# A hybrid block with a product-key expert layer on one core: the chosen experts' weights added into their table by GpSimd's indirect transfers

## The reference

```python
PEER_HEADS, PEER_N_KEYS, PEER_TOPK = 8, 128, 16      # 128 * 128 = 16384 experts

def peer_ffn(h, w_q, sub_keys, u_tab, v_tab):         # for 128 tokens hb at a time
    q = (hb @ w_q).reshape(128, 8, 2, 128)
    sc = jnp.einsum('thcd,hcnd->thcn', q, sub_keys)
    s1, i1 = lax.top_k(sc[:, :, 0], 16)
    s2, i2 = lax.top_k(sc[:, :, 1], 16)
    cand_s = s1[..., :, None] + s2[..., None, :]      # 256 candidates
    cand_i = i1[..., :, None] * 128 + i2[..., None, :]
    top_s, pos = lax.top_k(cand_s, 16)
    idx = jnp.take_along_axis(cand_i, pos, axis=-1)
    g = jax.nn.softmax(top_s, axis=-1)
    act = jax.nn.gelu(jnp.einsum('thkd,td->thk', u_tab[idx], hb))
    return jnp.einsum('thk,thkd->td', g * act, v_tab[idx])
```

## Time and profile before

| | us |
|---|---|
| median of 3 runs | 3407.14 |
| lowest, highest | 3405.34, 3407.44 |
| the profiled execution, its own time | 3407.45 |
| span of its trace | 3405.7 |
| PE busy | 3253.8 |
| DVE busy | 1926.9 |
| ACT busy | 1232.9 |
| POOL busy | 439.6 |

### The profile page before, as it was taken

One profiled execution on the slowest core, in us unless ns is written; L12 is line 12 of the kernel. 1 busy time (PEld: TensorE's weight loads), 2 busy tenths in 40 slices (PEclk: granted clock), 3 DMA queues, 4 the chain that ended last, 5 costly groups with the idle time before them and its releaser, 6 DMA issues.

```text
span 3405.7 us, 37836 instructions
## 1 busy us (share of the span) xinstructions
PE 3253.8 (96%) x14880; PEld 2663.0 (78%) x14880; DVE 1926.9 (57%) x3440; ACT 1232.9 (36%) x1770; POOL 439.6 (13%) x516
## 2 busy tenths in 40 slices
PE   7989999999999999999999999999999977899999
PEld 6767777778888878888788888887888855688887
DVE  5654444567777776665555555555444567544443
ACT  4663444432222235555322222223222233532221
POOL 0000000020000007885000000002000344030000
PEclk9999999899999999999999999999999986799999
DMA  4323111324443445778855555542333310022331
GB/s 139 92 87 100 56 56 56 126 93 129 143 137 126 129 135 158 191 197 204 295 194 195 194 198 198 198 148 75 99 99 99 115 62 13 13 74 99 99 99 62
DMA packets 271199, 424.21 MB, mean 125 GB/s; under 512 B 144816, under 2 KB 148400, under 8 KB 271024
## 3 DMA queue, kind: packets, MB, share of 16 engines
q1 hardware_dynamic: 271024, 421.80, 39.1%
HBM read 348.87 MB, written 72.88 MB: 124 GB/s over the span
## 4 chain that ended last, share of the span: by engine, by line
PE 86%; DVE 7%; ACT 5%; POOL 1%; issue 1%; DMA 1%; SPq 0%; POOLq 0%; ACTq 0%
PE pb L539 27%; PE pb L540 27%; PE pb L541 27%; PE pb L819 3%; ACT scr L1051 2%; DVE S L1486 1%; DVE ST L1494 1%; ACT S L1054 1%; DVE ST L1486 1%; DVE whl L1486 1%; ACT L1051 1%; POOL pad L2018 0%; POOL pad L2015 0%; ACT whl L1054 0%; DVE scr L1494 0%
## 5 line engine op out<-in xcount | busy, mean ns | idle before, releaser
L539 PE MATMUL pb<-H,whl 128*128 128x512 f32 x2416 | 992.2, 411 | 24.2 <-DVE whl L1486 11.6
L540 PE MATMUL pb<-H,whl 128*128 128x512 f32 x2416 | 953.7, 395 | 0.0
L541 PE MATMUL pb<-H,whl 128*128 128x512 f32 x2416 | 953.1, 394 | 0.0
L1486 DVE TENSOR_TENSOR whl<-raw,whl 128x1024 fp32r<-128x1024 f32 (+4 forms) x550 | 649.6, 1195 | 436.8 <-ACT whl L1054 434.7
L1054 ACT ACTIVATE whl<-raw 128x1024 fp32r<-128x1024 f32 (+4 forms) x550 | 543.9, 1003 | 466.2 <-PE pb L541 465.9
L539 PE MATMUL pb<-S,whl 128*128 128x512 f32 (+1 forms) x1716 | 670.2, 391 | 18.8 <-DVE whl L1486 11.7
L540 PE MATMUL pb<-S,whl 128*128 128x512 f32 (+1 forms) x1716 | 667.9, 389 | 0.0
L541 PE MATMUL pb<-S,whl 128*128 128x512 f32 (+1 forms) x1716 | 667.6, 389 | 0.0
L539 PEld LDWEIGHTS pb<-H,whl 128*128 128x128 f32 x2416 | 462.1, 191 | 117.5 <-DVE whl L1486 13.7
L541 PEld LDWEIGHTS pb<-H,whl 128*128 128x128 f32 x2416 | 460.8, 191 | 99.1
L540 PEld LDWEIGHTS pb<-H,whl 128*128 128x128 f32 x2416 | 462.5, 191 | 85.4 <-issue 3.4
(11 more groups left out here) (186 smaller groups left out, 2739.5 us busy)
## 6 DMA issues: line engine op xcount, KB each, us to landing
raw<-in_pu SPq DMA_DIRECT2D x128, 512.0 KB, 3.9
raw<-in_pv SPq DMA_DIRECT2D x128, 512.0 KB, 4.5
raw<-in_w_in SPq DMA_DIRECT2D x72, 512.0 KB, 3.7
ad<-scr SPq DMA_DIRECT2D x128, 256.0 KB, 4.2
gd<-ST SPq DMA_DIRECT2D x8, 4096.0 KB, 21.3
GA<-gd SPq DMA_DIRECT2D x60, 512.0 KB, 4.6
GA<-ad SPq DMA_DIRECT2D x60, 512.0 KB, 6.3
raw<-in_wg SPq DMA_DIRECT2D x44, 512.0 KB, 3.3
```

Of the source, the lines that this page charges most:

```text
L539: e.matmul(o, lh, h, start=start, stop=False, skip_group_check=True)
L540: e.matmul(o, lh, l, start=False, stop=False, skip_group_check=True)
L541: return e.matmul(o, ll, h, start=False, stop=stop, skip_group_check=True)
L1486: return e.tensor_tensor(o, x, y, op)
```

## The change

**The table.** `gd` is filled with zeros while the first attention runs: behind 32 of its weight loads SP issues a transfer of 1 MB of zeros from DRAM to DRAM. The steps `soft`, `over`, `rows`, `g` and `put` are gone. In their place a step `share` per head makes the softmax of that head (two subtractions and sums, one Exp on ACT, a reciprocal, a product) and, in `place`, the address of each chosen weight in `gd`. POOL then issues 64 indirect transfers per head, each of 128 numbers of four bytes, one per partition, that DRAM adds into `gd`; before the next head it waits until the last head's have landed.

**The order.** Queries and scores have two banks each (2 and 6, 3 and 7). Half of a head's work is moved behind the next head's queries: the step `sk` is now the product alone, `top` is the choice of the best 16 on DVE, and `lo` is DVE's low part of the query. A head takes 64 `u` steps, 8 of them between `pq` and `sk`, and `ga` comes behind 992. ACT calls `weights` of a `pq` behind the copy of the query's high part, not ahead of it. In `ffn("3")` the sum of squares is moved from the middle of `two` behind the next product.

```diff
+            if h < 7:
+                out.append(("pq", h + 1, c))
+            u(4)
+            out.append(("top", h, c))
+            if h < 7:
+                out.append(("lo", h + 1, c))
+            u(4)
+            if h < 7:
+                out.append(("sk", h + 1, c))
         for step in (("cand", h), ("best", h), ("pick", h, 0), ("pick", h, 1)):
             out.append(step)
-            u(8)
-    out.append(("soft",))
...
+            u(12)
+        out.append(("share", h))
...
# ScalarE, step pq
-                        weights("w_pq", n)
...
-                        copy(qh[c], bank[2]).then_inc(act.up(("pq_hi", n)), 1)
+                        copy(qh[c], bank[pq_bank[c]]).then_inc(act.up(("pq_hi", n)), 1)
+                        weights("w_pq", n)
...
# GpSimd
+            for h in range(8):
+                q.wait_ge(dve, ("shared", h))
+                if h:
+                    q.wait_ge(g_out[(h - 1) % 2], ("g", h - 1))
+                for b in range(4):
+                    for k in range(16):
+                        e.indirect_dma_start(g_rows, bass.IndirectOffsetOnAxis(ap=place[:, b, h, k:k + 1], axis=0),
+                                             TSv[:, b, h, k:k + 1], None, compute_op=ALU.add).then_inc(
+                            g_out[h % 2].up(("g", h)), 16)
...
# TensorE, ffn
-                            two(j, (bank[0], bank[2]), Hh, Hl, hx, (("gate", tag, 0), ("up", tag, 0)), tag)
+                            two(j, (bank[0], bank[2]), Hh, Hl, hx, (("gate", tag, 0), ("up", tag, 0)), tag if tag == "5" else None)
                             continue
                         linear(j, bank[i % 2], Hh, Hl, hx, ("gate", tag, i))
+                        if i == 1 and tag == "3":
+                            sum_of(tag)
```

More of the change, by code:

```diff
@@ L216, in u @@
             s += 1
+    out.append(("pq", 0, 0))
+    u(16)
+    out.append(("sk", 0, 0))
+    u(4)
+    out.append(("sk", 0, 1))
+    u(4)
     for h in range(8):
         for c in range(2):
[L220 to L223, removed]
-            u(8)
+            if h < 7:
+                out.append(("pq", h + 1, c))
+            u(4)
+            out.append(("top", h, c))
+            if h < 7:
+                out.append(("lo", h + 1, c))
+            u(4)
+            if h < 7:
+                out.append(("sk", h + 1, c))
         for step in (("cand", h), ("best", h), ("pick", h, 0), ("pick", h, 1)):
             out.append(step)
-            u(8)
-    out.append(("soft",))
[L229 to L244, removed]
+            u(12)
+        out.append(("share", h))
     u(8 * (124 - s // 8))
@@ L791, in experts @@
                         q.wait_ge(dve, ("pq", n))
-                        q.wait_ge(dve, ("top", n - 1) if n else ("bra", 7))
+                        q.wait_ge(dve, ("top", n - 2) if n > 1 else ("bra", 7))
+                        if n == 1:
+                            q.wait_ge(act, ("rstd", "2"))
                         for b in range(4):
                             t = slice(128 * b, 128 * b + 128)
-                            last = triple(bank[3][:, t], qh[c][:, t], ql[c][:, t], whi(j), wlo(j), True, True)
+                            last = triple(bank[sk_bank[c]][:, t], qh[c][:, t], ql[c][:, t], whi(j), wlo(j), True, True)
                         last.then_inc(prod.up(("w", j), ("sk", n)), 1)
[L797 to L809, removed]
-                        c = slice(128 * (k % 4), 128 * (k % 4) + 128)
-                        b = bank[gbank[n % 4]]
-                        if k % 4 == 0 and n > 3:
-                            q.wait_ge(act, ("put", n - 4))
-                        elif k == 0:
-                            q.wait_ge(dve, ("top", 15))
-                        if n % 4 < 3:
-                            q.wait_ge(pool, ("hot1", k))
-                        q.wait_ge(dve, ("hot2", k))
-                        last = e.matmul(b[:, c], hot2[n % 4][:, c], hot1[n % 4][:, c], start=True, stop=True, skip_group_check=True)
-                        if k % 4 == 3:
-                            last.then_inc(prod.up(("g", n)), 1)
                 for g in range(16):
@@ L836, in experts @@
                                             q.wait_ge(act, ("acts", 127))
[L837 to L838 removed]
+                                            q.wait_ge(dve, ("top", 15))
                                     r = slice(1024 * p + 512 * i, 1024 * p + 512 * i + 512)
@@ new lines, in experts @@
+                    elif what == "share":
+                        h = step[1]
+                        top, soft = TSv[:, :, h, :], share_of(h).rearrange("p (b k) -> p b k", b=4)
+                        total, at_ = sm_t[:, 0:4], ST[:, 3392:3456].rearrange("p (b k) -> p b k", b=4)
+                        then(tt(soft, top, TSv[:, :, h, 0:1].to_broadcast([128, 4, 16]), ALU.subtract), ("shifted", h))
+                        then(stt(at_, I1v[:, :, h, :], 128.0, I2v[:, :, h, :], ALU.mult, ALU.add))
+                        then(stt(at_, at_, 512.0, tok, ALU.mult, ALU.add))
+                        then(e.tensor_copy(place[:, :, h, :], at_))
+                        q.wait_ge(act, ("shares", h))
+                        then(e.tensor_reduce(total, soft, AX_X, ALU.add))
+                        then(e.reciprocal(total, total))
+                        then(tt(top, soft, total.unsqueeze(2).to_broadcast([128, 4, 16]), ALU.mult), ("shared", h))
```

106 lines of the change are left out of this document (37 added, 69 removed).

## The result

| | us |
|---|---|
| after, median of 4 runs | 3609.22 |
| lowest, highest | 3608.66, 3610.37 |
| before, median of 4 runs beside it | 3406.24 |
| ratio, with 95% interval | 1.0597, 1.0579 to 1.0616 |
| span of the trace after | 3608.5 |

All times are medians of the fast runs; one of e4's ten, 5247 us at a granted clock of 0.55, is a slow one and left out.

The account below looks back on a forecast made before the run. The prediction took PE, busy 3253.8 of 3405.7 us, as the bound: 3407.1 less 139 us of savings plus 122 us of stops ahead of `sk` gave 3390 us, range 3368 to 3530.

Parts of the forecast that it names:

- (h): POOL's 512 indirect transfers ahead of `ga`: 1.2 us each against a threshold of 1.53, so in time and costing nothing.
- The transfers come late: Rival, chance 0.21: POOL's issue above 1.53 us each stops PE ahead of `pv`; 3477 us at 1.7, 3579 at 1.9.
- Each transfer pays its whole way: Rival, chance 0.08: POOL's transfers run one behind the other at 2.0 us, 240 us late, giving 3630 us.
- POOL's work slows DVE: Rival, chance 0.08: each of two low parts in a stop ahead of `sk` loses 1.5 us, 42 in all; 3432 us.
- (f): Between query and scores, PE waits for DVE's `lo`: 14 stops of 6.8 us ahead of `sk`, 122 us with slow clock.
- term for the clock: Slow products behind each stop ahead of `sk`: 1.9 us each, 14 times, 27 us.
- The terms that go: Savings from one-hot products, `over`, `soft`, the start of `pv` and ffn("3"): together 139.2 us.
- (e): In ffn("3"), moving the sum of squares removes PE's 6.25 us gap and 2.0 of slow work: 8.2 us saved.
- (d): At the start of `pv`, PE's wait goes because `ga` stands 32 `u` steps ahead, with slow products: 5.1 us saved.
- (g): Clearing `gd` by 32 transfers of 1 MB, some 4 us each, costs nothing; 128 us if the cover failed.
- likeliest case: The forecast itself, stops of 6.8 us and transfers in time: 3390 us, chance 0.58, own range 3372 to 3410.

Follow-up runs that it names:

- e4: Kernel after with 256 of 512 transfers, and ACT splitting a query step's weights ahead of the query's high-part copy, as before the change: 3397.16 us, ratio to before 0.9971.
- e6: Kernel after with its 512 adding indirect transfers carrying 64 numbers instead of 128: 3544.34 us.
- e10: Kernel after with 512 indirect transfers that write instead of adding and carry 64 numbers instead of 128: 3411.36 us.
- e2: Kernel after with 256 of 512 transfers and `top` ahead of the next head's query, 80 `u` steps a head: 3279.73 us, ratio to before 0.9629.
- e1: Kernel after with 8 of each head's 16 chosen experts in the table, 256 indirect transfers instead of 512: 3411.32 us, ratio to before 1.0014.
- e8: Kernel after with the table divided, blocks 0 and 1 by 256 transfers, 2 and 3 by 256 one-hot products, `top` ahead of the next query: 3343.55 us, ratio 0.9815.

## Why the prediction was wrong

**The step that failed is (h), the price of one indirect transfer.** The threshold was named (1.53 us) and the place where lateness would show (one piece ahead of `pv`, released through SP's loads) as well. The value was 1.2, where 1.95 was measured in the same terms (1.98 with the waits at the heads). It came from POOL's own row of 0.60 us over 128 numbers, doubled for two descriptors each. Both halves of that were wrong: e6 shows that the numbers are 0.12 us per 64, and e10 and e6 that most of the price is there at 64 numbers already (0.90 writing, 0.52 more adding), which no row of arithmetic over 128 numbers could tell. The upper bound, 1.9 from the landing of SP's smallest load, was no bound: the price was just above it, and it belongs to another engine's kind of transfer. The range closed at 3530, at 1.8 us each, inside the rival; it should have reached at least to that rival's own end, 3579, and even that lies under 3609. Put 1.95 into the prediction's own sum and it gives 3390 + 0.42 x 512 = 3605, 4 us from the result. That is partly luck: the 3390 is 21 too low, as shown below, and the lateness would be 215 us where 198 was measured.

**The rivals.** *The transfers come late* is what happened, 0.21 by my chances. *Each transfer pays its whole way* came near the number (2.0) by another mechanism: if POOL waited for each landing, its row would show DMA as what ended its idle time 511 times, and it does so 6 times, 15.9 us in all. POOL is busy 1.54 us with each. Its queue's packets take 6.3% of 16 engines' span, some 22% of the 1012 us in which it runs, so the engines that move the data had room; whether a full queue ever holds POOL was not tested. The Trainium skill ("Perfetto Trace Analysis", DMA Instruction — SWDGE (GPSIMD)) says that the profile's end of such an instruction is the end of the making of its descriptors, not the landing; the trace agrees: the last row ends at 1839.77, and SP's load, which waits for the landing, starts at 1841.19. The other page that the prediction used (the Trainium skill, "DMA: Bandwidth & Descriptors", Anatomy of one DMA) calls the making small beside the receipt; here, with transfers of 512 bytes issued one behind the other, the measured 1.54 us decides, and the wait for a receipt comes once a head.

*POOL's work slows DVE* is wrong: two low parts took 2.36 us in the stop, 1.18 each, and the stops are 94.4 us with 512 transfers and with 256. It is the other way round. With all else idle (1660 to 1840 us) and beside a busy DVE (1100 to 1300), the same line of after is (count, busy us, mean ns):

```profile
L1995 POOL DMA_INDIRECT gd<-scr,place x95 | 146.5, 1542 | 34.0 <-issue 31.8 <-DMA gd<-scr,place 2.1
```
```profile
L1995 POOL DMA_INDIRECT gd<-scr,place x100 | 166.0, 1660 | 34.2 <-issue 32.1 <-DMA gd<-scr,place 2.1
```

The long ones are those that start inside a DVE operation with two inputs in SBUF, most often a low part:

```profile
1286.04 1.23 DVE L1459 TENSOR_TENSOR whl<-raw,whl 128x1024 fp32r<-128x1024 f32 x1 [0.26 <-ACT whl L1033]
```
```profile
1286.10 2.57 POOL L1995 DMA_INDIRECT gd<-scr,place  x1 [0.30 <-issue]
```

DVE's row ends at 1287.27 and POOL's 1.40 us later. So it is throughout: 68 of the 512 took more than 1.6 us, and all but one of these, the very first transfer, start inside such an operation and end 1.38 to 1.42 us behind its end. Those that start inside any other DVE operation took 1.54 to 1.59. In nine cases a transfer started within 0.04 us behind a low part; then it kept its 1.54, and the low part took 1.27 to 1.30 us; the other low parts kept 1.22 or 1.23. This is the rule that the prediction weighed (the Trainium skill, "SBUF — State Buffer", Who interferes with whom), on POOL's side, to which it gave no price; it makes 35 of the 1014 us that the 512 transfers took. The same section of the Trainium skill infers that the making of descriptors is not held by such an operation; here it was held, 67 times.

**Step (f), the stops,** was right in cause, number and length: 14 stops of 6.7 to 6.8 us, taken away by e2 and shortened by e4 to 5.6. Its term for the clock was small: 1.9 was taken "since part of the slow time falls on the short products of `sk`", but a short product loses as well (1.20 us on twelve, and 1.29 on the six behind them, so 2.5). By e1 and e2 it is 2.7 to 3.0 on average. That is 11 to 15 us on 122; the measured sum is 131.6. Nor is it one price by length: single stops of 6.7 to 6.8 us lose 2.3 to 3.6 us behind them.

**The terms that go** came to 127.4 us (before 3407.1, e2 3279.7) where the sum had 139.2. (e) is 7.4 instead of 8.2. (d) failed: the wait at `pv` is still 2.94 in e1, after 3.68. It was read as waiting for the loads, which were issued 19.4 us ahead; but in e1 they are issued 23.5 ahead, and PE waits for this chain:

```profile
1659.61 0.60 ACT L1030 ACTIVATE scr<-pb 128x512 f32<-128x512 f32 x1 [3.89 <-PE pb L542]
...
1660.10 1.05 ACT L1033 ACTIVATE S<-ST 128x1024 fp32r<-128x1024 f32 x1
...
1661.18 1.23 DVE L1459 TENSOR_TENSOR S<-ST,S 128x1024 fp32r<-128x1024 f32 x1 [3.07 <-ACT S L1033]
...
1662.51 0.47 PE L540 MATMUL pb<-S,whl 128*128 128x512 f32 x1 [2.94 <-DVE S L1459]
```

ACT makes the first high part only behind the gelu of the last bank of `u`, so this wait is ACT's order, not a load. Nor did the slow products go for certain: behind this stop of 2.94 us e1 loses 0.1 us (granted clock 1.00 from 1662 to 1672 us), and e2 behind a stop of the same length 3.0 (0.66 from 1531 to 1541), where before lost 1.7 behind 3.68. The eight waits for `whl` in e2, 7.2 us, were not in the sum. With (d) at -0.6 as in e2, (e) at 7.4 and these, it would have been some 126.

**Step (g), the clearing,** was right. From 320 to 400 us, before and after (PE, PEld, DVE, ACT, POOL busy, then clock, DMA share, GB/s):

```profile
320.00:400.00 80.00, 74.88 (x354) 56.89 (x354) 38.66 (x85) 38.41 (x81) 0.00 (x0) 0.96 0.20 58
```
```profile
320.00:400.00 80.00, 74.91 (x354) 56.94 (x354) 38.69 (x84) 38.38 (x81) 0.00 (x0) 0.96 0.46 165
```

The DMA share goes from 0.20 to 0.46 and PE doesn't move.

So without (h) the kernel is at 3411, where 3390 was forecast: 11.8 us less went than the sum had, and 9.6 more came. That is equal to before within 0.2%, not faster, and just outside the 3372 to 3410 that the prediction gave to its likeliest case.

## What to carry to other kernels

A sum over many small transfers hangs on one price, so where no row has that price, take its threshold, and let the chances and the range go by how far apart the bounds are rather than by a value in between; a price of one engine's transfers is no bound for another's. Divide work between two engines by their measured prices and the time that each has (e8), instead of moving all of it to the one that looks idle: here a one-hot product costs PE 0.25 us, and the transfer that replaces it costs POOL 2.0, but POOL's first 400 or so are free. And a gain on one engine is worth nothing while another sets the end: the same new order was worth 132 us with half the transfers and 4 with all.

## What the hardware showed that was not expected

- An adding indirect transfer of 128 numbers of four bytes keeps POOL busy 1.54 us and leaves 0.30 between two. A writing one takes 0.96. Half of the numbers saves 0.12 and 0.06.
- The adding form has 144 packets for 128 numbers (80 for 64, 48 for 32), the writing form 32 for 128 and for 64.
- A transfer that starts inside a DVE operation with two inputs in SBUF ends 1.38 to 1.42 us behind the end of that operation (67 cases in after), so it takes up to 2.58 us instead of 1.54. DVE's low parts lost at most 0.07 us, in the nine cases in which both start together.
- After a stop of 6.8 us the products of 128 columns are slow as well, 0.22 us instead of 0.12, and the stop costs 2.3 to 3.6 us more than its length. Two stops of 2.94 us cost 0.1 (e1) and 3.0 us (e2) more.
- One wait in SP's list held, for 201.7 us, also a store that another engine needed: ACT stood 201.11 us until it had landed.
